# First projection of the decay gate with high and low weights side by side in one stationary tile

## The reference, cut to what matters

```python
h = rmsnorm(x, norm_mix[l])
q, k, v, r = jnp.split(h @ w_in, [dk, 2 * dk, 2 * dk + dv], axis=-1)
log_a = jax.nn.log_sigmoid(((h @ w_a1) @ w_a2 + b_a).astype(jnp.float32)) / GLA_TAU
```

## Time and profile before

| | |
|---|---|
| runs of the whole program | 2612.4, 2610.0, 2610.16 us, median 2610.16 |
| span of the profiled execution, first to last instruction | 2603.8 us; its own device time is not recorded beside it |
| busy share PE / DVE / ACT / POOL | 97% / 63% / 40% / 30% |
| mean granted PE clock | 0.999 |
| instructions | 44426, of which PE 18590 matmuls |
| DMA | 252.26 MB, 97 GB/s |
| chain that ended last | PE 79%, DVE 12%, issue 3%, ACT 2%, DMA 2%, POOL 1% |

### The profile page before, as it was taken

One profiled execution on the slowest core, in us unless ns is written; L12 is line 12 of the kernel. 1 busy time (PEld: TensorE's weight loads), 2 busy tenths in 40 slices (PEclk: granted clock), 3 DMA queues, 4 the chain that ended last, 5 costly groups with the idle time before them and its releaser, 6 DMA issues.

```text
span 2603.8 us, 44426 instructions
## 1 busy us (share of the span) xinstructions
PE 2535.8 (97%) x18590; PEld 2453.8 (94%) x18590; DVE 1644.9 (63%) x2628; ACT 1051.4 (40%) x1727; POOL 790.8 (30%) x524
## 2 busy tenths in 40 slices
PE   8999999999999999999999999999999999999999
PEld 6999999999999999999998998899999999999999
DVE  6735353569766765774725786555697666748754
ACT  6333333364332333332437676445453323333312
POOL 5131212152444434002522214323334443440002
PEclk9999999999999999999999999999999999999999
DMA  3111111132323335452213444132223333336522
GB/s 111 35 37 35 37 35 37 35 104 74 116 91 115 103 99 197 132 170 78 61 35 112 144 175 148 55 100 69 67 72 99 108 99 108 114 113 229 166 70 90
DMA packets 229682, 252.26 MB, mean 97 GB/s; under 512 B 16849, under 2 KB 178271, under 8 KB 228591
## 3 DMA queue, kind: packets, MB, share of 16 engines
q1 hardware_dynamic: 227087, 247.36, 29.0%
q10 hardware_dynamic: 2400, 2.10, 0.3%
HBM read 173.54 MB, written 75.89 MB: 96 GB/s over the span
## 4 chain that ended last, share of the span: by engine, by line
PE 79%; DVE 12%; issue 3%; ACT 2%; DMA 2%; POOL 1%; SPq 0%; DVEq 0%; ACTq 0%; POOLq 0%
PE ps L897 13%; PE ps L899 13%; PE ps L898 13%; PE ps L345 9%; PE ps L347 8%; PE ps L346 8%; PE ps L2772 3%; PE ps L1687 1%; PE ps L2756 1%; PE ps L1674 1%; PE ps L1676 1%; PE ps L1675 1%; DVE hflat L490 1%; PE ps L1763 1%; PE ps L1746 1%
## 5 line engine op out<-in xcount | busy, mean ns | idle before, releaser
L1559 POOL TENSOR_TENSOR wlo<-wraw,whi 128x1024 fp32r<-128x1024 f32 x78 | 192.4, 2467 | 440.1 <-DVE s_raw L1250 440.1
L310 POOL TENSOR_TENSOR wlo<-wraw,whi 128x2048 fp32r<-128x2048 f32 (+1 forms) x21 | 94.3, 4489 | 591.9 <-ACT whi L303 562.5
L897 PE MATMUL ps<-hh,whi 128*128 128x264 f32 x928 | 264.6, 285 | 4.0 <-DVE hf L1327 2.3
L899 PE MATMUL ps<-hh,wlo 128*128 128x264 f32 x928 | 263.9, 284 | 0.0
L898 PE MATMUL ps<-hl,whi 128*128 128x264 f32 x928 | 263.9, 284 | 0.0
L345 PE MATMUL ps<-hh,whi 128*128 128x352 f32 x648 | 218.5, 337 | 0.6 <-ACT cqr L3091 0.3
L347 PE MATMUL ps<-hh,wlo 128*128 128x352 f32 x648 | 208.0, 321 | 0.0
L346 PE MATMUL ps<-hl,whi 128*128 128x352 f32 x648 | 207.8, 321 | 0.0
L589 DVE TENSOR_TENSOR xT<-xT,ps 128x352 f32<-128x352 f32 x288 | 147.1, 517 | 86.4 <-PE ps L347 85.2
L897 PEld LDWEIGHTS ps<-hh,whi 128*128 128x128 f32 x928 | 174.6, 188 | 5.4 <-DVE hf L1327 2.7
L1559 POOL TENSOR_TENSOR s_lo<-s_raw,s_hi 128x512 fp32r<-128x512 f32 x80 | 158.0, 1975 | 60.1 <-DVE wlo L1291 30.1
(11 more groups left out here) (458 smaller groups left out, 8678.5 us busy)
## 6 DMA issues: line engine op xcount, KB each, us to landing
wraw<-w_ffn_in SPq DMA_DIRECT2D x88, 512.0 KB, 3.9
s_a<-hf SPq DMA_DIRECT2D x44, 528.0 KB, 3.5
wraw<-w_ffn_out SPq DMA_DIRECT2D x44, 512.0 KB, 4.1
s_t<-h SPq DMA_DIRECT2D x16, 1056.0 KB, 4.5
hflat<-s_t SPq DMA_DIRECT2D x16, 1056.0 KB, 6.3
h<-s_a SPq DMA_DIRECT2D x12, 1056.0 KB, 5.7
wraw<-w_gla_in SPq DMA_DIRECT2D x24, 512.0 KB, 4.5
s_x<-xT SPq DMA_DIRECT2D x6, 1408.0 KB, 5.5
```

Source lines behind the costliest of these rows:

```text
L310: pool.tensor_tensor(lo[:, 0:cols], raw[:, 0:cols], hi[:, 0:cols].bitcast(F32), ALU.subtract).then_inc(S("w_lo"), 1)
L897: nc.tensor.matmul(out, w_[0], x_[0], start=first, stop=False, skip_group_check=True)
L899: last = nc.tensor.matmul(out, w_[1], x_[0], start=False, stop=(k == HK - 1), skip_group_check=True)
L1559: return pool.tensor_tensor(lo[:, cols], raw[:, cols], hi[:, cols].bitcast(F32), ALU.subtract)
```

## The change

The high and low parts of `w_a1` go side by side into one tile `a1s` of 32 columns per `k`. One pass with `hh` gives 32 result rows, t from the high weights in rows 0 to 15 and t from the low weights in rows 16 to 31; a second pass with `hl` and the high weights adds to rows 0 to 15. So a slice takes 16 matmuls, not 24. The halves are added by the second projection: `zs` now has 96 rows (high of both halves, low of both halves, high of both again) and `za` holds six copies of `w_a2`. The low product of the second half is computed too.

With all 96 rows filled no zeros are needed: DVE's memset of `za` and POOL's of `zs` go, and with them the waits on them. ACT's queue issues six DMAs for `za`, not three. `t_copy(0)` waits for the last turned x (`x_mm`), whose tile lies under `zs`. ACT and POOL write `a1s` with a stride.

```diff
--- before.py
+++ after.py
@@ -143,10 +143,8 @@
         sq0a = at("sq0a", [P, KD // 2, TC], W)
         sq0b = at("sq0b", [P, KD // 2, TC], R + 9 * D + 12 * P)
         pmix = at("pmix", [2 * KD, P], R + 9 * D + 12 * P + KD * TC)
-        a1raw = at("a1raw", [P, KD * GRANK], R + 8 * T + 19 * DV + 4 * T)
-        a1lo = at("a1lo", [P, KD * GRANK], R + 8 * T + 19 * DV + 4 * T, F32R)
-        a1hi = at("a1hi", [P, KD * GRANK], R + 8 * T + 19 * DV + 4 * T + KD * GRANK, F32R)
-        A1 = (a1hi, a1raw, a1lo)
+        a1raw = at("a1raw", [P, KD, GRANK], R + 8 * T + 19 * DV + 4 * T)
+        a1s = at("a1s", [P, KD, 2 * GRANK], R + 8 * T + 19 * DV + 4 * T + KD * GRANK, F32R)
 
 
         gq = at("gq", [P, 2, T], R)
@@ -164,7 +162,7 @@
         gS = at("gS", [P, 9, DV], R + 8 * T + 10 * DV)
         gb = at("gb", [P, GH, T], R + 8 * T + 19 * DV)
 
-        ZK = 5 * GRANK
+        ZK = 6 * GRANK
         za = at("za", [ZK, GH * DK], R + 9 * D + 4 * P)
         zah = at("zah", [ZK, GH * DK], R + 9 * D + 8 * P, F32R)
         zs = at("zs", [ZK, T], R + 6 * T, F32R)
@@ -272,7 +270,7 @@
                   "summed": ("z_min", 12), "t_sum": ("z_log", 12), "s_sum": ("z_scan", 12), "t_lo_dve": ("qb", GH),
                   "s_lo": ("o_pair", NCH * GH), "first_lo": ("x_mm", 18), "x_spilled": ("s0_loaded", 16 * GH),
                   "a_stored0": ("x_loaded0", 48), "a_stored1": ("x_loaded1", 48), "a_loaded0": ("x_loaded2", 48),
-                  "a_loaded1": ("mix_loaded", 16), "x_back0": ("rows", 17 * 16), "x_back1": ("consts_late", 16 * 5),
+                  "a_loaded1": ("mix_loaded", 16), "x_back0": ("rows", 17 * 16), "x_back1": ("consts_late", 16 * 8),
                   "t_stored": ("consts", 32)}
 
         def nth(name, n):
@@ -1634,11 +1632,14 @@
 
         def pe_gla_t(pe, j):
 
-            wv = views((a1hi, a1lo), 0, KD, GRANK)
             for k in range(KD):
                 row_ready(pe, 0, j, k)
-                last = mm3(ps[0:GRANK, B_BANKS[j], 0:TC], [v[:, k, :] for v in wv],
-                           (hh[:, k, tc(j)], hl[:, k, tc(j)]), k == 0, k == KD - 1)
+                if k == KD - 1:
+                    pe.matmul(ps[0:GRANK, B_BANKS[j], 0:TC], a1s[:, k, 0:GRANK], hl[:, k, tc(j)], start=False, stop=False)
+                last = pe.matmul(ps[0:2 * GRANK, B_BANKS[j], 0:TC], a1s[:, k, :], hh[:, k, tc(j)],
+                                 start=(k == 0), stop=(k == KD - 1))
+                if k < KD - 1:
+                    pe.matmul(ps[0:GRANK, B_BANKS[j], 0:TC], a1s[:, k, 0:GRANK], hl[:, k, tc(j)], start=False, stop=False)
             last.then_inc(S("t_mm"), 1)
 
         def pe_gla_z(pe, j, heads):
@@ -1847,9 +1848,9 @@
             def t_copy(j):
                 act.wait_ge(S("t_mm"), j + 1)
                 if j == 0:
-                    act.wait_ge(S("z_mask"), 1)
+                    act.wait_ge(S("x_mm"), 2 * (NG + 1))
                 for r_ in (0, 4):
-                    last = act.activation(zs[r_ * GRANK:(r_ + 1) * GRANK, tc(j)], ps[0:GRANK, B_BANKS[j], 0:TC], ACT.Copy)
+                    last = act.activation(zs[r_ * GRANK:(r_ + 2) * GRANK, tc(j)], ps[0:2 * GRANK, B_BANKS[j], 0:TC], ACT.Copy)
                 last.then_inc(S("t_sb"), 1)
 
             def z_abs(j, h):
@@ -2118,8 +2119,8 @@
 
             def t_low(j):
                 dve.wait_ge(S("t_sb"), 2 * j + 1)
-                dve.tensor_tensor(zs[2 * GRANK:3 * GRANK, tc(j)], ps[0:GRANK, B_BANKS[j], 0:TC],
-                                  zs[0:GRANK, tc(j)].bitcast(F32), ALU.subtract).then_inc(S("t_sb"), 1)
+                dve.tensor_tensor(zs[2 * GRANK:4 * GRANK, tc(j)], ps[0:2 * GRANK, B_BANKS[j], 0:TC],
+                                  zs[0:2 * GRANK, tc(j)].bitcast(F32), ALU.subtract).then_inc(S("t_sb"), 1)
 
             def z_min(j, h):
                 dve.wait_ge(S("z_abs"), GH * j + h + 1)
@@ -2135,11 +2136,11 @@
             def z_scan(j, h):
                 u = GH * j + h
                 dve.wait_ge(S("z_log"), u + 1)
-                dve.wait_ge(S("z_mask"), 4)
+                dve.wait_ge(S("z_mask"), 3)
                 dve.tensor_tensor_scan(gb[:, h, scan_cols(j)], zcm[:, scan_cols(j)], gb[:, h, scan_cols(j)], 0.0,
                                        ALU.mult, ALU.add).then_inc(S("z_scan"), 1)
 
-            low = slice(4 * GRANK, 5 * GRANK)
+            low = slice(4 * GRANK, 6 * GRANK)
             dve.wait_ge(S("za_sb"), 1)
             dve.tensor_tensor(zah[low, :], za[low, :], zah[low, :].bitcast(F32), ALU.subtract).then_inc(S("za_sb"), 1)
             dve.wait_ge(S("par_mm"), 2)
@@ -2202,15 +2203,15 @@
                         .then_inc(S("sq0_pair"), 1)
 
             x_pairs(0)
-            pool_split(pool, chunk(0), KD * GRANK, A1)
+            pool.wait_ge(S("w_hi"), 1)
+            pool.tensor_tensor(a1s[:, :, GRANK:2 * GRANK], a1raw[:, :, :], a1s[:, :, 0:GRANK].bitcast(F32),
+                               ALU.subtract).then_inc(S("w_lo"), 1)
             pool_split(pool, gc(0, 0), WC)
             norm_out_pool(pool, 0, [0])
-            pool.wait_ge(S("x_mm"), 2 * (NG + 1))
-            pool.memset(zs[:, :].bitcast(F32), 0.0).then_inc(S("z_mask"), 1)
             x_pairs(2)
             pool.wait_ge(S("par_mm"), 2)
             pool.memset(zcm[:, :], 1.0).then_inc(S("z_mask"), 1)
-            pool.wait_ge(S("z_mask"), 2)
+            pool.wait_ge(S("z_mask"), 1)
             pool.memset(zcm[:, 0:SEQ].rearrange("p (g t) -> p g t", t=GRP)[:, :, 0:1], 0.0).then_inc(S("z_mask"), 1)
             pool.memset(zcm[:, SEQ:SEQ + 1], 0.0).then_inc(S("z_mask"), 1)
             norm_out_pool(pool, 0, [1, 2])
@@ -3389,13 +3390,13 @@
 
             x_load(range(3))
             sp.dma_start(pmix[:, :], A["norm_mix"].rearrange("l (k p) -> (l k) p", p=P)).then_inc(S("mix_loaded"), 16)
-            sp_load(sp, chunk(0), halves(a1raw[:, :].rearrange("p (k n) -> p k n", k=KD),
+            sp_load(sp, chunk(0), halves(a1raw[:, :, :],
                                          A["w_gla_a1"][0].rearrange("(k p) n -> p k n", p=P)))
             x_load(range(3, 6))
             sp_gla_qk(sp, 0)
             x_load(range(6, 9))
 
-            sp.wait_ge(S("prow_zero"), 2)
+            sp.wait_ge(S("prow_zero"), 1)
 
             def row(tile, r, src):
                 n, w = src.shape
@@ -3468,22 +3469,22 @@
             act.dma_start(ones[:, :], A["c_mats"][:, P:2 * P]).then_inc(S("consts"), 16)
             act.dma_start(rot[:, :], A["c_mats"][:, 2 * P:3 * P]).then_inc(S("consts_late"), 16)
             act.dma_start(masks[:, :], A["c_masks"]).then_inc(S("consts_late"), 16)
-            act.wait_ge(S("prow_zero"), 1)
-            for r_ in (0, 2, 4):
+            for r_ in range(6):
                 act.dma_start(za[r_ * GRANK:(r_ + 1) * GRANK, :], A["w_gla_a2"][0]).then_inc(S("consts_late"), 16)
 
 
             log_exp_table(act)
 
             x_squares(act, 0, range(KD))
-            act_split(act, chunk(0), KD * GRANK, A1)
+            act.wait_ge(S("w_loaded0"), 32)
+            act.activation(a1s[:, :, 0:GRANK], a1raw[:, :, :], ACT.Copy).then_inc(S("w_hi"), 1)
             act_split(act, chunk(1), WC)
             x_squares(act, 1, range(4))
             x_root_act(act, 0)
             x_squares(act, 1, range(4, KD))
             norm_out_act(act, 0, [0])
             x_root_act(act, 1)
-            act.wait_ge(S("consts_late"), 16 * 5)
+            act.wait_ge(S("consts_late"), 16 * 8)
             act.activation(zah[:, :], za[:, :], ACT.Copy).then_inc(S("za_sb"), 1)
             act_gla(act)
             act.wait_ge(S("state_out"), 32 * GH + 16)
@@ -3499,7 +3500,6 @@
 
         @block.vector
         def _(dve):
-            dve.memset(za[:, :], 0.0).then_inc(S("prow_zero"), 1)
             dve.memset(prow[:, :, :], 0.0).then_inc(S("prow_zero"), 1)
             dve.memset(scrap[:, 1:2], 0.0).then_inc(S("state_out"), 16)
             dve.memset(epsc[:, :], EPS).then_inc(S("down_added"), 2)
```

## The result

The changed kernel took **2617.31 us** (median of 7 runs, 2613.11 to 2622.66) where the kernel before took 2611.36 in the same comparison (7 runs, 2609.18 to 2614.01): a recorded ratio of 1.0030, 95% interval 1.0021 to 1.0040. (The ratio of the two medians alone is 1.0023, at the lower end of that interval; the text gives the recorded ratios.) It is slower by 0.2 to 0.4%, and outside the forecast range. The profiled execution is the slowest of the seven, 2622.66 us, with a span of 2620.8, so the 17 us between the two profiled spans say less than the medians.

A forecast was written before the change was run, and what follows sets the result against it. It took a road through DVE's norms, `L1795`, `whi`, `wlo` and the scan to bound the kernel, not PE. 0 for the matmuls, + 2.81 + 0.24 = +3.05 us on 2610.16 gave 2613.2 us, range 2608.3 to 2616.0.

The forecast's parts named there:

- POOL first, clock kept: Likeliest case: POOL leads DVE in slice 1's `hl`, full clock stays; 2613.2 us (2612 to 2614), chance 0.40.
- the slow clock: Rival: POOL first, and PE's clock falls to half behind its longer waits; 2614.9 to 2616.6 us, chance 0.20.
- What the 24 matmuls are worth: 0: Gate, slices 0 to 2: 3.83 us of PE work removed, gaining nothing because other engines' roads cover it.
- All three covers: PE's waits for DVE ahead of the `prow` transposes, z of slice 0's third head and z of slice 1.
- The order on the port: +2.81: Norm of slice 1: POOL's `hl` issued 0.25 us ahead of DVE's, so DVE's four take turns; cost 2.81 us.
- Three more DMAs: +0.24, bound twice that: Start, ACT's queue: 96 KB more at 410 GB/s delay `w_gla_in` by 0.24 us, between 0 and twice that.
- The clock, at nothing: Sum held no clock loss; the rival put 1.7 us on z and `L1795` behind PE's longer wait.
- as much again: Clock rival's second part: PE's hole at 74.56 grows by a microsecond and may cost as much again, giving 2616.6.
- The base: Start of the sum: 2610.16 us, the median of three times of the kernel before.
- launch and end: Whole kernel: the 6.4 us by which the median 2610.16 lies above the profiled span of 2603.8.
- A shift at 78 us stays to the end: Behind the gate: a delay there lasts to the kernel's end, since later loads and waits hang on one another.
- Slower by over 0.2%: 0.13: Whole kernel: chance of 0.13 for slower by over 0.2% (limit 2615.4), some two thirds of the slow-clock case.

The follow-up runs named there:

- e5: The change with POOL made to wait for DVE's `hl` of slice 1 and the six `za` loads moved behind x on SP's queue: 2612.64 us, ratio 1.0009.
- e13: The changed kernel run again as it is, in a second comparison: 2621.42 us (5 runs), ratio 1.0035.
- e3: The change, with POOL made to wait until DVE's four `hl` of slice 1 are through: 2615.19 us, ratio 1.0016.
- e6: Kernel before, all 24 matmuls a slice, POOL doing its `hl` of slice 1 ahead of its `zcm` memsets: 2610.45 us, ratio 1.0006.
- e1: Kernel before with 16 a1 matmuls a slice (product of `hh` with the low weights left out), nothing else changed: 2616.33 us, ratio 1.0025.
- e2: Kernel before with six instead of three loads of the gate's second weight on ACT's queue: 2610.33 us, ratio 0.9999.
- e4: The change with the six `za` loads moved from ACT's queue to SP's, behind x: 2617.84 us (6 runs), ratio 1.0030.
- e10: The change with 20 matmuls of unused result in PE's hole ahead of the levels (`L1706`): 2614.40 us, ratio 1.0027.
- e7: The change with 16 matmuls of unused result in PE's hole at 43 us: 2616.85 us, ratio 1.0029.
- e9: Kernel before with 20 matmuls of unused result ahead of the levels of head 0 (`L1705`): 2606.94 us, ratio 0.9992.
- e11: e8 with ACT's high part of chunk 1 moved ahead of the soft part of slice 0: 2604.51 us, ratio 0.9984.
- e12: e9 with ACT's high part of chunk 1 moved ahead of the soft part of slice 0: 2606.66 us, ratio 0.9993.
- e14: The change with both fillers, that of e7 and that of e10: 2613.58 us, ratio 1.0018.
- e15: e14 with the six `za` loads behind x on SP's queue: 2611.55 us, ratio 1.0003.
- e8: e5 with 20 matmuls of unused result in PE's hole ahead of the levels of head 0 (`L1706`): 2606.65 us, ratio 0.9993.

## Why the prediction was wrong

The step that failed is the clock. The sum priced waits only and put the lower clock behind the longer holes at nothing ("POOL first, clock kept", 0.40, with the slow clock a rival at 0.20). The first 92 us of the change's trace show +1.61 us behind the hole at 43 and +2.4 at the levels in its place. What idle time it takes for the clock to fall is not shown. The second fault is of size: the three loads stood in the sum with 0.24 us and cost 0.93 in this trace. The forecast direction of the sum, its path and its largest term were right.

- **What the 24 matmuls are worth: 0.** Right as far as the levels. All three covers were there: holes of 1.75 us (1.7 forecast), 2.82 (2.8) and 1.04 (1.2). Slice 2 ended as forecast, behind `wlo`: the scan was stretched to 3.53 us, and e5's scans end within 0.12 us of before's. But the work was costed at nothing only up to that point, and the next place was passed over, where PE waits for DVE again. There PE's head start turns up as a hole of 2.94 us instead of 1.70, and the second level falls 1.1 us (e5, e13) to 2.4 us (the change) further behind the first.
- **The order on the port: +2.81.** Right: the lead is 0.25 us, the turns cost 2.78. e3 and e6 show it from both sides, and e1 shows what sets it off. The Trainium skill, "SBUF — State Buffer", section "Who interferes with whom", says that a DVE instruction with two SBUF inputs contends with a GpSimd one that reads SBUF, and that the issue order decides which of them blocks. The traces agree (DVE's four `hl` take 4.60 us in turns, 1.82 alone), and add what follows when both have four to do: with POOL ahead by 0.25 us they alternate, with DVE ahead, in e2 by 0.06 us, DVE goes through and POOL waits.
- **Three more DMAs: +0.24, bound twice that.** This term was mis-sized. They cost 0.93 us in the change, 0.83 in e2 alone, e4 takes 0.95 back, and the mean over all traces is 0.67. I priced bytes by a rate of 410 GB/s. The stretches of the change, then of before (columns as in the earlier trace rows), show another one, with the DMA engines as busy:

```profile
9.00:10.00 1.00, 1.00 (x7) 1.00 (x6) 0.74 (x2) 0.00 (x0) 0.00 (x0) 1.00 0.94 232
10.00:11.00 1.00, 1.00 (x7) 1.00 (x6) 0.84 (x2) 0.00 (x0) 0.00 (x0) 1.00 1.05 330
```
```profile
9.00:10.00 1.00, 1.00 (x7) 1.00 (x6) 0.84 (x2) 0.00 (x0) 0.00 (x0) 1.00 0.99 393
10.00:11.00 1.00, 1.00 (x8) 1.00 (x7) 0.84 (x2) 0.00 (x0) 0.00 (x0) 1.00 1.03 414
```

  From 9 to 11 us the seven traces with six loads on ACT's queue move 232 to 348 GB/s and the ten others 373 to 426, at the same busy share. As far as these rows show, the price is the time that the loads hold the DMA engines, not their bytes; the bound from above had to come from a stretch in which such loads were moved.
- **The clock, at nothing.** This is the step that failed. The fall of the clock was a rival with its mechanism and 1.7 us for the hole at 43 (measured 1.61), and "as much again" for the hole at 74.56 (measured 2.4). Its case came to 2616.6 at most, with 0.20; with 0.93 instead of 0.24 for the loads it would have said 2617.3. I held against it that the gap was 0.4 us shorter and had no small matmuls in it. The runs do not bear that out: in every trace here with an unfilled hole of 2.1 to 2.8 us at that place (the change, e1, e4, e6, e10, e13) the clock fell behind it, and in none with the hole filled or absent (before, e2, e3, e5, e7 to e9, e11, e12, e14, e15). The trace of before could have said so: it has a second fall, at 103 us, and in the 20 us ahead of that PE never idled for more than 0.85 us (PE's timeline, then the stretch):

```profile
100.38 2.00 PE L1687 MATMUL ps<-gqd,gkd 128*128 128x64 f32 x16 [0.85 <-DVE gkd L2026]
```
```profile
103.00:106.00 3.00, 3.00 (x16) 0.50 0.00 0
```

- **The base.** 1.20 us of the miss are not the change's: the sum starts from 2610.16, the median of three runs, and before's median over seven is 2611.36. Counted as a difference the range ends at +5.84 and the first comparison has +5.95, just outside, while the second has +10.94, far outside. The 6.4 us called "launch and end" were misread, though the sum does not rest on them: in every run whose span is on record the time is 1.7 to 3.3 us above its span, and the profiled execution was a faster one than the median.
- **A shift at 78 us stays to the end.** No run shows this. e6 is 3.97 us late at the first level, 2.44 at 205 us and 1.3 in the medians; falls of the clock that come or stay away in between are as large as the shift.
- **Slower by over 0.2%: 0.13.** This was too low by the same step, since it was taken as two thirds of the clock's case.

## What to carry to other kernels

Count what PE does not do any more twice: once as time saved on a road, and once as idle time ahead of the next join. If a hole like those here (2.1 to 2.9 us) opens or grows ahead of matmuls on the critical road, put the lower clock into the likeliest case, once for each such hole. And where two engines that share the SBUF port reach their part within a few tenths of a us of each other, fix the order with a wait (e3) before removing work ahead of either.

## What was not expected of the hardware

- 20 matmuls whose result nobody reads, 2.5 us of PE work, make e5 faster by some 4 us (e8). In the kernel before they show 2 us, which is not clear of noise (e9, 0.9992, interval to 1.0001). Filled or not decided the clock at the levels in 16 of 17 traces, with 16 matmuls a slice as with 24.
- A filled hole does not keep the clock with certainty: in e14 the granted clock was 0.50 from 81.7 to 88.5 us behind an idle time of 0.57 and 1.06 us; in e15, with the same PE code 0.4 us earlier, it was 1.00. Nor does a fall need a long hole, as the one at 103 us before shows.
- One 16-row load of 32 KB is worth 0.2 to 0.3 us of everyone else's landing in that stretch (0.67 to 0.95 us for three), three to four times what its bytes take at 410 GB/s.
- With a few us of scatter from the clock, effects of 1 us can only be read in the traces' early part. Of the two fills the runs show 1.0029 and 1.0027 one at a time and 1.0018 together, against 1.0030 and 1.0035 for the change: that they add up is as possible as that only both together help.
